# Feed-forward products of a two-block network by Strassen's algorithm, seven block products for eight

## What is computed

```python
# D_MODEL = 1024, SEQ = 512, D_FF = 2816
def swiglu(u, w_gate, w_up, w_down):
    return (jax.nn.silu(u @ w_gate) * (u @ w_up)) @ w_down
...
    h = h + hybrid_mixer(rmsnorm(h, attn_norm_g[l]), pos, topk, ...)
    h = h + swiglu(rmsnorm(h, ffn_norm_g[l]), w_gate[l], w_up[l], w_down[l])
h = rmsnorm(h, final_norm_g)
```

## Time and profile before

| | |
|---|---|
| Runs | 1665.81, 1668.92 and 1669.39 us, median 1668.92 us |
| Profiled execution, first to last instruction (span) | 1664.5 us |
| PE busy | 1625.8 us, 98% of the span |
| DVE, ACT, POOL busy | 1003.7, 713.9 and 474.9 us |

### The profile page before, as it was taken

The page is one execution under the profiler, slowest core; times in us unless marked ns, Lnnn a source line. Parts: engine busy times, 40 slices in busy tenths (PEclk is TensorE's granted clock), DMA queues, the critical chain, the costliest instruction groups (busy, mean ns, idle before and its releaser), DMA issues.

```text
span 1664.5 us, 24805 instructions
## 1 busy us (share of the span) xinstructions
PE 1625.8 (98%) x10072; PEld 1296.2 (78%) x10072; DVE 1003.7 (60%) x1569; ACT 713.9 (43%) x1112; POOL 474.9 (29%) x169
## 2 busy tenths in 40 slices
PE   9999999999999998999999999999999999999998
PEld 7778688888778786778887886786778888888887
DVE  4356635786999999984672755998963212222123
ACT  4482433334555567655433333327763322222122
POOL 2221124342000000000434431234773344344332
PEclk9999999999999999999999999999999999999999
DMA  5232013235655454556643321221003333322322
GB/s 177 77 101 76 27 52 99 79 101 162 141 145 142 123 150 114 119 137 212 225 134 115 101 74 52 76 57 52 1 1 102 92 86 101 101 80 80 99 87 86
DMA packets 268311, 167.98 MB, mean 101 GB/s; under 512 B 90811, under 2 KB 248854, under 8 KB 268070
## 3 DMA queue, kind: packets, MB, share of 16 engines
q1 hardware_dynamic: 256592, 146.45, 31.6%
q10 hardware_dynamic: 11158, 18.08, 3.2%
q0 software_dynamic: 448, 1.88, 0.3%
HBM read 144.87 MB, written 16.78 MB: 97 GB/s over the span
## 4 chain that ended last, share of the span: by engine, by line
PE 82%; DVE 9%; SPq 3%; ACT 3%; issue 1%; DMA 1%; ACTq 0%; DVEq 0%
PE PS L728 23%; PE PS L729 23%; PE PS L730 23%; SPq L2945 2%; SPq L2955 1%; PE PS L1365 1%; PE PA L957 1%; DVE ring_lo L2162 1%; PE PS L1353 1%; PE PA L981 1%; PE PA L1315 1%; PE PA L1194 1%; PE PA L985 1%; PE PA L1080 1%; DMA KM<-GS 1%
## 5 line engine op out<-in xcount | busy, mean ns | idle before, releaser
L2890 POOL TENSOR_TENSOR ring_lo<-ring,ring_hi 128x2048 fp32r<-128x2048 f32 (+2 forms) x90 | 393.8, 4376 | 1103.7 <-ACT ring_hi L1515 1101.2
L1515 ACT ACTIVATE ring_hi<-ring 128x2048 fp32r<-128x2048 f32 (+2 forms) x121 | 221.0, 1827 | 205.9 <-PE PS L730 167.7
L729 PE MATMUL PS<-U3l,ring_hi 128*128 128x512 f32 x352 | 139.9, 397 | 0.0
L728 PE MATMUL PS<-U3h,ring_hi 128*128 128x512 f32 x352 | 139.4, 396 | 0.0
L730 PE MATMUL PS<-U3h,ring_lo 128*128 128x512 f32 x352 | 138.9, 395 | 0.0
L2833 DVE TENSOR_TENSOR SF<-PS,rs 128x512 f32<-128x512 f32 x22 | 15.2, 691 | 162.7 <-PE PS L730 162.7
L728 PE MATMUL PS<-HT5h,ring_hi 128*128 128x512 f32 x256 | 105.5, 412 | 0.0
L730 PE MATMUL PS<-HT5h,ring_lo 128*128 128x512 f32 x256 | 101.4, 396 | 0.0
L729 PE MATMUL PS<-HT5l,ring_hi 128*128 128x512 f32 x256 | 101.2, 395 | 0.0
L2063 ACT ACTIVATE SF<-SF 128x512 f32<-128x512 f32 x22 | 13.9, 631 | 171.1 <-DVE SF L2833 171.1
L2162 DVE TENSOR_TENSOR ring_lo<-ring,ring_hi 128x2048 fp32r<-128x2048 f32 x31 | 70.5, 2286 | 18.6 <-ACT ring_hi L1515 18.5
(11 more groups left out here) (509 smaller groups left out, 4091.6 us busy)
## 6 DMA issues: line engine op xcount, KB each, us to landing
ring<-in_gla_w_in SPq DMA_DIRECT2D x20, 1024.0 KB, 5.2
ring<-in_s_w_in SPq DMA_DIRECT2D x16, 1024.0 KB, 6.0
ring<-in_s_w_glu SPq DMA_DIRECT2D x16, 1024.0 KB, 5.8
ring<-in_w_gate SPq DMA_DIRECT2D x22, 512.0 KB, 4.0
ring<-in_w_up SPq DMA_DIRECT2D x22, 512.0 KB, 5.2
ring<-in_w_down SPq DMA_DIRECT2D x16, 704.0 KB, 4.5
ring<-in_w_in SPq DMA_DIRECT2D x9, 1024.0 KB, 5.2
ring<-in_gla_w_out SPq DMA_DIRECT2D x8, 1024.0 KB, 5.6
```

Source lines behind the costliest of these rows:

```text
L728: pe.matmul(dst, w[0], x[0], start=start, stop=False)
L729: pe.matmul(dst, w[0], x[1], start=False, stop=False)
L1515: act.activation(ring_hi[:, n % NSLOT, 0:plan.size[n]], ring[:, n % NSLOT, 0:plan.size[n]], ACT.Copy)\
L2890: pool.tensor_tensor(ring_lo[:, n % NSLOT, at], ring[:, n % NSLOT, at], ring_hi[:, n % NSLOT, at].bitcast(F32), ALU.subtract).then_inc(wlo ...
```

## The change

Both feed-forward products are done by the Winograd form of Strassen's algorithm on blocks of 2 by 2. A block of weights is 128 features by 2 times 128 output columns, a block of the input 2 times 128 features by 256 tokens. Seven block products take the place of eight, each of them with sums of weight blocks and of input blocks as its operands, and its results are added up to four output blocks.

- The work is cut into *groups*, each two output tiles by the 512 tokens (for `ffn_up` the gate tile i and the up tile i, 22 groups; for `ffn_down` two tiles of the output over eight of the 22 hidden tiles, four groups in each of two phases). A group is two *units*. A unit has 1024 columns of raw weights, from which seven blocks of 256 columns (1792 columns, in the buffer `WS`) come: three raw, and four sums made in place by DVE in three instructions. There are 60 units.
- A unit is 7 x 2 products, or 42 matmuls of 256 columns. Four of the seven sums are complete in PSUM only after the second unit, and DVE adds them up in the buffer `E` (four instructions with a PSUM input each, after one copy by ACT).
- ACT writes the high parts of a unit to `WV` in two instructions (768 and 1024 columns), POOL the low parts over `WS` in two (the same sizes). POOL waits for the sums of DVE with both. `WS` has five buffers, `WV` three.
- The inputs get the same sums: for each pair of tiles three additions by DVE, then one high part by ACT and one low part by DVE, of 1792 columns each.
- For hidden tiles below 16 the scaling of the up half by `rs1` moves behind the down product, where DVE multiplies 1024 columns by `rs1` and adds 1024 columns to `XT` for each group.
- The last six hidden tiles of `ffn_down` are multiplied as before, eight tiles of 18 matmuls of 512 columns, with four loads of 1536 columns of weights, the last tile again in halves.
- DVE makes the sums of the first five units, and POOL and ACT work on the first three, within and just after `attn_out`.

```diff
+    side_by_side("up", 0, 1)
+    ups(2, PHASE + 1)
+    for phase in range(2):
+        side_by_side(("down", phase), 0, 1)
...
+PRODUCTS = ((0, W_A11, X_B11, True, True), (6, W_A22, X_T4, True, False), (1, W_A12, X_B21, True, False), (2, W_S2, X_T2, False, True),
+            (3, W_S1, X_T1, True, False), (4, W_S3, X_T3, False, True), (5, W_S4, X_B22, False, True))
+PHASE = 8
+NW, NV = 5, 3
...
@@ pe_program @@
+                for i, (at, block, xblock, opens, ends) in enumerate(PRODUCTS):
+                    if i in (0, 3):
+                        pe.wait_ge(unit_low, UNIT_LOW + 2 * u.n + (1 if i == 0 else 2))
+                    for j in range(2):
...
+                        m = product(half_bank(g.bank, at), (hi[:, here], lo_[:, here]), (blocks(x[0], xblock, 1), blocks(x[2], xblock, 1)),
+                                    opens and u.half == 0 and j == 0, ends and u.half == 1 and j == 1)
...
@@ dve_program @@
+            def outcome(g):
...
+                dve.wait_ge(first_copied, FIRST_COPIED + g.n + 1)
+                dve.wait_ge(ended, ENDED + ENDINGS * g.n + 2)
+                tt(pair[:, 0:4:3, :], twice(blocks(E, 4, 1)), two(bank_pair(g.bank, 0)), ALU.add).then_inc(first_added, 1)
+                if n is not None:
+                    first = unit_first_sums(n)
+                dve.wait_ge(ended, ENDED + ENDINGS * g.n + 3)
...
+                at = count(tt(two(blocks(E, 1, 2)), twice(blocks(E, 3, 1)), two(bank_pair(g.bank, 1)), ALU.add))
+                if n is not None:
+                    second = unit_second_sum(n, first)
+                dve.wait_ge(ended, ENDED + ENDINGS * g.n + 4)
...
+                at = count(tt(blocks(E, 3, 1), blocks(E, 2, 1), half_bank(g.bank, 3), ALU.add))
+                if n is not None:
+                    unit_third_sum(n, second)
...
+                tt(blocks(E, 1, 2), blocks(E, 1, 2), bank_pair(g.bank, 2), ALU.add).then_inc(bank_free, 1)
...
@@ pool_program @@
+            for n in range(len(units)):
+                (raw, lo_), hi = WS[n % NW], WV[n % NV]
+                parts = ((0, 3), (3, 7)) if n < SPLIT_UNITS else ((0, ENDS),)
+                for i, (first, stop) in enumerate(parts):
+                    if n < SPLIT_UNITS:
+                        pool.wait_ge(sums_ready, SUMS + n + 1)
+                    pool.wait_ge(unit_high, UNIT_HIGH + unit_parts(n) + i + 1)
+                    pool.tensor_tensor(blocks(lo_, *part), blocks(raw, *part), blocks(hi, *part).bitcast(F32), ALU.subtract)\
+                        .then_inc(unit_low, 1)
```

More of the change, by code:

```diff
@@ L259, in build, with open_group, unit, ups @@
     pairs("attn_out", wo3, 0, KD)
[L260 to L264, removed]
-    tiles = plan.tiles
+    tiles = plan.tiles
+    units, groups = [], []
+    def open_group(kind, i):
+        groups.append(Group(kind, i, len(groups)))
+        return groups[-1]
+    def unit(group, half):
+        units.append(Unit(group, half, len(units)))
+        if half == 1:
+            group.last = units[-1].n
+    def ups(first, stop):
+        for i in range(first, stop):
+            g = open_group("up", i)
+            unit(g, 0)
+            unit(g, 1)
+    def side_by_side(kind, i, j):
+        pair = [open_group(kind, i), open_group(kind, j)]
+        for half in range(2):
+            for g in pair:
+                unit(g, half)
+    side_by_side("up", 0, 1)
+    ups(2, PHASE + 1)
+    for phase in range(2):
+        side_by_side(("down", phase), 0, 1)
+        for f in (2, 3):
+            g = open_group(("down", phase), f)
+            unit(g, 0)
+            unit(g, 1)
+        ups((phase + 1) * PHASE + 1, min((phase + 2) * PHASE + 1, KF))
+    SPLIT_UNITS = len(units)
+    for f in range(KD // 2):
+        units.append(Unit(None, f, len(units)))
+    for g in groups:
+        g.after = next((h.last for h in groups if h.last > g.last), g.last)
+    ENDS = KF - 2 * PHASE
+    DOWN_LAST = [max(g.last for g in groups if g.kind == ("down", phase)) for phase in range(2)]
     DVE_LOADS.append(tiles["ks"][0].loads[0])
-    HALVES = [t.loads[0] for stage in ("gla_v", "vs", "ffn_down") for t in tiles[stage] if plan.last_use[t.loads[0]] == t.t]
+    HALVES = [t.loads[0] for stage in ("gla_v", "vs") for t in tiles[stage] if plan.last_use[t.loads[0]] == t.t]
     NORMS, norm_at = {}, [0, 0]
@@ L1397, in to_tokens @@
+            for u in units[:SPLIT_UNITS]:
+                unit_products(u)
+                if u.n == 0:
+                    read_out(pe, tiles["attn_out"][-1])
+                    norm_rows("ffn", T, PS[:, 2, :])
             def to_tokens(i):
                 pe.wait_ge(fo_ready, i + 1)
+                if i == 0:
+                    pe.wait_ge(bank_free, BANK_FREE + len(groups))
                 if i == 4:
@@ L2080, in act_program @@
             link(act.activation(warm[:], con[:, C_EPS:C_EPS + 1], ACT.Sqrt))
-            last = tiles["ffn_down"][-1]
             s0, n0, _ = NORMS["fin2"]
```

502 lines of the change are left out of this document (376 added, 126 removed).

## The result

The changed kernel takes 1783.95 us (median; 1782.78 to 1786.68) against 1669.16 us: 1.069 times as long, with a 95% interval of 1.0675 to 1.0705. It is 115 us slower; the forecast was 1770, and the time lies in its range. The profiled execution spans 1781.0 us.

The account below looks back on a forecast made before the run. PE bounds the kernel before; after the change DVE and POOL, excluding each other, were to bound the groups. 1282 + 5 + 450 - 8 + 28 + 9 = 1766 us of span, plus 4.4, gave 1770 us; range 1690 to 1850.

Parts of the forecast that it names:

- The group: Feed-forward groups: 15.2 us each in ffn_up, 14.5 in ffn_down, 450 us for all thirty.
- 8.7 + 8.5 - 2.0: One ffn_up group: DVE's work plus POOL's subtractions, less 2.0 us overlap, of which 1.5 for PSUM additions beside POOL.
- The bound of 13.4: Least time of an ffn_up group: POOL's 8.5 us plus 4.9 us in which DVE's SBUF instructions hold; 12.9 in ffn_down.
- The passes: DVE's thirty passes over the groups: 450 us, with -8 us for late beginning, sums made ahead and end loads.
- The start: First feed-forward products, delayed by extra DVE work in attn_out: 5 us later, between 0 and 12.
- The end: After the last pass: 28 us for last hidden tile, six matmuls and six tiles, then 9 us of tail.
- The sum: Whole kernel: 1282 + 5 + 450 - 8 + 28 + 9 = 1766 us of span, plus 4.4 to the median.
- PE stays the bound: Feed-forward groups: DVE and POOL don't delay each other, a group takes 10.0 us, time 1633; chance 0.08.
- Tightly packed: Feed-forward groups: overheads and PSUM additions vanish beside POOL, groups of 13.4 and 12.9 us, 1675 to 1715; chance 0.09.
- The clock: Feed-forward groups: waits drop PE to half clock, 20.0 us of PE a group, 1845 to 1920 us; chance 0.13.
- What would show it: Signs in ffn_up: PE busy 65%, 15 us between silus, DVE nearly always busy, POOL pieces over 1.85 and 2.40.
- The rule that was weighed: Shared SBUF ports: two-input VectorE and SBUF-reading GpSimd operations lock each other out; with it no group under 13.4 us.

Follow-up runs that it names:

- The fill: Changed kernel with POOL filling the low parts of the weights with zeros instead of subtracting: 1641.12 us, 0.984 of the kernel before.
- the one-input form: Changed kernel with POOL multiplying raw weights by 1 into the low parts, one SBUF input instead of two: 1660.84 us, 0.996 of the kernel before.
- the low parts on DVE: Changed kernel with DVE making the weights' low parts, POOL nothing, plus two reorderings at start and end: 1693.16 us, 1.015 of the kernel before.
- the reordering: Changed kernel with DVE's sums of the fourth unit moved behind the input norm's last squares in attn_out: 1783.10 us, 1.0698 of the kernel before.

## Why the prediction was right, point by point

**The mechanism.** It named DVE and POOL excluding each other as what sets the time. The fill, the one-input form and the low parts on DVE show it from three sides: take away POOL's two-input subtraction and the group falls from 14.8 to 9.9, 10.1 or 12.0 us. Taking away DVE's side of it, the sums, gives 12.2.

**The group, 15.2 forecast, 14.8 measured; in `ffn_down` 14.5 and 13.3.** The sum was 8.7 + 8.5 - 2.0. Measured, it is 7.8 + 8.5 - 1.5. DVE's own part was too high, since it added the durations shown, and rows of DVE overlap (`L3137` at 1408.62 shows 0.68, and the next starts 0.60 after it). The part that runs beside POOL is 1.5 us, the amount that the forecast gave to the PSUM additions, though not by them alone: of the four, only `L3137` runs wholly beside a subtraction in the group shown, `L3151` does for its last 0.5 us (1412.98 against POOL's start at 1413.14), and I take the rest to lie in the starts and ends of instructions that follow each other across the engines. The other 0.5 of the 2.0 was the overlap of rows again, counted for the blocked ones only. The bound of 13.4 wasn't reached, since POOL's pair is released by the sums (`L3070`), and then a row of SBUF inputs is what DVE has next, not its PSUM additions. In `ffn_down` the miss is larger, 1.2 us: a group's rows take 7.4 us in the kernel with fills (1401.02 to 1408.43), and 7.4 + 8.5 - 13.3 = 2.6 us run beside POOL, since there `L3137` and `L3142` both fall into subtractions (1469.06 and 1470.92, with POOL at work from 1467.69 to 1473.25). So the 15.2 is as near as it is partly by luck: DVE's part was 0.9 too high and the overlap 0.5 too high, and they offset each other.

The list of rows ahead has a slip that the sum doesn't share: a group that makes the input sums of a pair has fifteen rows on DVE, not fourteen. The sum counted them.

**The passes.** From the first addition on `E` to the last hidden tile the forecast had 1300 to 1729, 429 us; it was 1311.65 to 1733.1, 421.5 us. The shorter groups gave 22 x 0.4 + 8 x 1.2 = 18 us. Some 11 of them were spent at two places that the sum didn't have, the turns from `ffn_up` to `ffn_down`. Some of PE's waits, there and elsewhere (engine, what it writes, line, what it waited for: us in total, times, longest); the largest total, 16.9 us in seven waits ahead of other groups, has no releaser in the trace:

```profile
PE PS L881 <- DVE Hl3r L3127: 15.8, 2, 8.0
PE PA L881 <- DVE E L3151: 15.1, 2, 7.6
PE PS L968 <- DVE ssq L2360: 13.1, 1, 13.1
PE PA L881 <- DVE Hl1r L3123: 8.6, 2, 8.2
```

At each turn PE waits 7.6 us for a PSUM bank, which comes free at `L3151`, and soon after 8 us for the low part of the last hidden pair, which the down products need at once. Then it goes on at half clock: the granted clock is 0.50 from 1443.2 to 1448.3 us and from 1620.5 to 1625.5, the matmuls of 256 columns step by 0.213 us for 0.119, and DVE idles for 5.0 us until the group is through. Four groups of 13.3 and one of 14.8 would be 68.0 us from `SF` to `SF`; the two turns show 72.9 and 73.7, so they cost 5 to 6 us each, of which the half clock makes some 2.3 (24 steps of 0.094).

**The start, 5 us forecast in a bound of 0 to 12.** The first addition on `E` came at 1311.65 where the forecast had 1282 + 5 + 13 = 1300, 12 us later. The first 24 matmuls of the part are early, at 1280.0 us, and then PE stands for the 13.1 us of the row above. The sums of squares for the norm stand behind a unit's weight sums in DVE's order, and these were blocked by POOL's first units. Timeline of DVE:

```profile
1290.13 2.29 DVE L3060 TENSOR_TENSOR WS<-WS 128x512 f32<-128x512 f32 x1
...
1295.29 0.68 DVE L2360 TENSOR_TENSOR ssq<-ssq,sq 128x512 f32<-128x512 f32 x1
...
1302.16 0.69 DVE L3113 COPY rs<-PS 128x512 f32<-128x512 f32 x1 [4.45 <-PE PS L974]
```

The exclusion that the forecast charged to each group wasn't charged to the start. The order of these rows is 3.5 us of it, as the reordering showed. Another 2 us are PE's clock: after the wait it is granted 0.50 from 1297 to 1301 us, and DVE then idles 1.92 us for PE before the first addition on `E`.

**The end, 28 + 9 forecast, 47.9 measured** (1733.1 to 1781.0). Timeline rows of POOL, DVE and PE, and two stretches in windows:

```profile
1727.93 3.86 POOL L3275 TENSOR_TENSOR WS2r<-WS,WV2r 128x1536 fp32r<-128x1536 f32 x1
1728.44 3.90 DVE L3162 TENSOR_TENSOR E<-E,rs 128x512 f32<-128x512 f32 x1
...
1733.85 0.79 PE L881 MATMUL PA<-Hh1r,WV0r 128*128 128x512 f32 x1 [8.25 <-DVE Hl1r L3123]
...
1735.30 0.63 PE L881 MATMUL PA<-Hh0r,WV0r 128*128 128x512 f32 x1
1735.72 0.63 PE L882 MATMUL PA<-Hl0r,WV0r 128*128 128x512 f32 x1
...
1734.00:1744.00 10.00, 9.82 (x32) 7.57 (x33) 2.72 (x5) 1.98 (x3) 0.41 (x1) 0.75 0.00 0
1744.00:1781.00 37.00, 28.77 (x176) 24.25 (x174) 17.33 (x27) 11.29 (x21) 3.08 (x1) 0.89 0.15 58
```

Two steps failed. The forecast had six matmuls between the last low part and the six remaining tiles; there are 24, since the second tile doesn't start ahead of it (18 x 0.2345 = 4.2 us more). And after its wait of 8.25 us PE goes on at half clock for twelve matmuls: they step by 0.42 us instead of 0.2345 and take 5.2 us (1733.85 to 1739.04) for 2.8, 2.4 us more. From 1740 to 1770 us the clock is 1.00 again; the 0.89 of the second row comes from the tail behind 1770, where PE is busy for 2.8 of 11 us, so it isn't a cost of the tiles. What the sum left out there are the transposes to tokens that stand between the tiles (L1582): from 1742.16 to 1770.42 it is 28.3 us for the 25.3 of six tiles. The tail after the last product took 10.6 us for 9, and the last low part 0.5 less than counted.

**The sum.** Start +11.6, passes -7.5 and end +10.9 against the forecast's steps give +15: 1766 + 15 = 1781, the span. From the span to the median it is 3.0 us, not 4.4, so the median is 14 us off. Each error is small beside 115 us, and the first points up in part because the exclusion was costed in the passes alone. That the passes came out shorter while start and end came out longer is luck.

**The rivals.** *PE stays the bound* (1633) is what the fill shows at 1641: PE's saving is real, and POOL's subtraction takes it away. *Tightly packed* (13.4): the groups lie between it and the forecast, near the forecast in `ffn_up` (14.8, between 13.4 and 15.2) and near this rival in `ffn_down` (13.3, between 12.9 and 14.5). *The clock*: below full in every stretch of the passes, 0.90 to 0.99. In single groups of `ffn_up` it costs nothing: those from 1339.89 and 1575.51 have 1.00 and last 14.72 and 14.73 us, those from 1398.98 and 1545.98 have 0.88 and last 14.71 each, since DVE's turn-taking leaves room for it. Where PE is what is waited for, behind waits of 7.7 to 13.1 us, it did cost something: some 2 us at the start, at each turn and at the end, 9 us in all. The Trainium skill (TensorE: Matmul & The Clock Gate, section "HAM oscillation — how this bites in real kernels") tells of a kernel whose waits between bursts bring the clock down at each step; the trace agrees that the clock drops behind waits, and shows that it costs nothing while another engine is later.

**What would show it.** PE busy 65%: 69 and 72 in `ffn_up`. Some 15 us from silu to silu: 14.8. DVE busy nearly all the time: 98.8. `E` additions at 0.69: all. POOL's pieces longer than 1.85 and 2.40: together 10.0 us a group (67.79 in 6.8 groups) for 8.5, blocked by DVE in turn. The sign for the clock was a value below 0.9 in this stretch: it is 0.94 and 0.90.

**The rule that was weighed** held for this kernel, though not in all its words. The Trainium skill (SBUF — State Buffer, section "SBUF: two separate sides") has a GpSimd operation that reads SBUF and a VectorE operation with two SBUF inputs exclude each other for the whole instruction. With POOL's two inputs the trace agrees (2.88 us for 0.69). With one input it depends on the size: beside copies of 768 and 1024 columns, of 2.1 us and more, some 0.8 us are lost at most, and groups of 10.1 us have POOL busy for 99.5% of the time; beside one of 1536 columns an addition takes 3.58 us for 0.69. The measurement decides.

## What to carry to other kernels

Before work is given to an engine that looks idle, ask which instructions of its neighbour it will stand in the way of. Here DVE at 23% and POOL at 42% of `ffn_up` looked like room for both, but their two-input instructions add up in time: price a POOL subtraction of two SBUF operands at its full POOL duration on DVE's path (2.14 ns a column, against DVE's own 1.1), unless DVE has PSUM work just then. A busy share doesn't show this: DVE was as "busy" with POOL's help as without, and did fewer groups; only durations against those of the same size elsewhere show it. And when PE's work is cut by an eighth, count the vector work that pays for it: DVE's 12.0 us a group were more than PE's 10.0 even in the best version that computes everything.

## What the runs showed of the hardware that I had not expected

- POOL with one SBUF input (2.1 us for 768 columns, 2.8 for 1024, slower than the subtraction's 1.85 and 2.40) delays a DVE addition of two SBUF inputs by up to 0.85 us, and by nothing where it starts 0.9 us or later into the copy. A copy of 1536 columns (4.25 us) holds it until 0.33 us before the copy's end. With two inputs POOL holds it for the whole instruction at every size here.
- Fills are free on both sides: 0.74 us for 768 columns on POOL with DVE's sums at 0.68, and 0.48 us for 512 on DVE beside POOL's subtraction.
- DVE additions on the same buffer `E`, one right behind another, start 0.1 to 0.2 us later than when an independent instruction stands between them (0.78 us for 0.60). In the interleaved order that time is free for a sum.
- PE was granted half clock (0.50) for 4 to 5 us behind waits of 7.7 to 13.1 us, and 0.88 on average in some groups of `ffn_up`, where its waits are 1 to 3 us. The first cost some 2 us each time, the second nothing (14.71 us a group for 14.72). What it would cost in a kernel that PE bounds stays open.
